# The moving operand of the split matmuls read as two interleaved halves, with weight columns stored even ones first

## The reference

```python
h = rms_norm(x) @ w_ff1            # 1024 -> 4096
x = x + square(relu(h)) @ w_ff2    # 4096 -> 1024
```

```python
def swiglu_ffn(h, w_gu, w_down):
    a, b = jnp.split(h @ w_gu, 2, axis=-1)   # 1024 -> 2 x 2816
    return (jax.nn.silu(a) * b) @ w_down     # 2816 -> 1024
```

## Time and profile before

| | |
|---|---|
| median of 3 runs | 1878.97 us (1878.77 to 1880.35) |
| profiled execution, its own time | 1878.69 us |
| its span | 1876.9 us |
| matmul records | 9754, each with a weight load |
| TensorE, weight loads, VectorE, ScalarE, GpSimd busy | 1868.9, 1591.5, 1420.3, 901.9, 222.7 us |
| HBM traffic | 190 GB/s over the span |

### The profile page before, as it was taken

How to read it: one execution, slowest core, us unless ns; L and a number is a source line. 1 busy time by engine, 2 the same in 40 slices (tenths; PEclk the granted TensorE clock), 3 DMA queues, 4 the chain that set the end, 5 groups by cost and what they waited for, 6 DMA issues and landing times.

```text
span 1876.9 us, 25424 instructions
## 1 busy us (share of the span) xinstructions
PE 1868.9 (100%) x9754; PEld 1591.5 (85%) x9754; DVE 1420.3 (76%) x1621; ACT 901.9 (48%) x990; POOL 222.7 (12%) x189
## 2 busy tenths in 40 slices
PE   9999999999999999999999999999999999999998
PEld 7888888888888888888898888888888898888887
DVE  7997866579868666776789887667766789887666
ACT  5564443444644344534545545444444555545443
POOL 0000000000001000000058230000000058230000
PEclk9999999999999999999999999999999999999999
DMA  8555555564556554555465456555655465455552
GB/s 305 191 178 209 181 193 188 179 216 180 185 199 222 192 193 165 213 191 189 157 194 180 164 198 225 186 191 182 213 183 186 172 194 180 157 202 207 187 182 109
DMA packets 52016, 357.40 MB, mean 190 GB/s; under 512 B 6552, under 2 KB 6688, under 8 KB 10080
## 3 DMA queue, kind: packets, MB, share of 16 engines
q1 hardware_dynamic: 47952, 341.93, 52.0%
q0 software_dynamic: 3696, 14.33, 2.6%
q10 hardware_dynamic: 288, 0.04, 0.0%
HBM read 354.15 MB, written 2.11 MB: 190 GB/s over the span
## 4 chain that ended last, share of the span: by engine, by line
PE 99%; issue 0%; DMA 0%; DVE 0%; ACT 0%; DVEq 0%; POOLq 0%; POOL 0%; SPq 0%; ACTq 0%
PE ps L234 24%; PE ps L309 14%; PE ps L310 14%; PE ps L317 14%; PE ps L239 13%; PE ps L196 4%; PE ps L198 3%; PE ps L197 3%; PE ps L2894 1%; PE ps L2895 1%; PE ps L2899 1%; PE ps L2639 1%; PE ps L214 0%; PE ps L221 0%; PE ps L215 0%; PE ps L413 0%
## 5 line engine op out<-in xcount | busy, mean ns | idle before, releaser
L172 DVE TENSOR_TENSOR w_lo<-raw,w_hi 128x2048 fp32r<-128x2048 f32 x312 | 716.5, 2302 | 239.4 <-ACT w_hi L165 238.5
L165 ACT ACTIVATE w_hi<-raw 128x2048 fp32r<-128x2048 f32 x312 | 596.8, 1915 | 499.3 <-PE ps L317 239.8
L234 PE MATMUL ps<-a,w_hi 128*128 128x512 f32 x2016 | 479.8, 390 | 0.0
L234 PEld LDWEIGHTS ps<-a,w_hi 128*128 128x128 f32 x2016 | 374.5, 188 | 75.4
L239 PEld LDWEIGHTS ps<-a,w_lo 128*128 128x128 f32 x2016 | 258.5, 191 | 9.8
L239 PE MATMUL ps<-a,w_lo 128*128 128x256 f32 x2016 | 261.5, 283 | 0.0
L309 PE MATMUL ps<-w_hi,a 128*128 128x512 f32 x592 | 233.2, 394 | 0.0
L310 PE MATMUL ps<-w_hi,a 128*128 128x512 f32 x592 | 230.6, 390 | 0.0
L309 PE MATMUL ps<-w_hi,mix 128*128 128x512 f32 x576 | 225.1, 391 | 0.0
L310 PE MATMUL ps<-w_hi,mix 128*128 128x512 f32 x576 | 225.0, 391 | 0.0
L317 PE MATMUL ps<-w_lo,a 128*128 128x512 f32 x592 | 146.3, 389 | 0.0
(11 more groups left out here) (416 smaller groups left out, 2065.2 us busy)
## 6 DMA issues: line engine op xcount, KB each, us to landing
raw<-in_w_b SPq DMA_DIRECT2D x198, 1024.0 KB, 4.8
raw<-in_w_a SPq DMA_DIRECT2D x124, 1024.0 KB, 4.9
rows<-in_post_gains POOLq DMA_DIRECT2D x6, 512.0 KB, 6.0
rows<-in_rows_a POOLq DMA_DIRECT2D x2, 1028.0 KB, 7.8
raw<-in_w_a SPq DMA_DIRECT2D x4, 512.0 KB, 6.8
rows<-in_rows_a POOLq DMA_DIRECT2D x2, 1024.0 KB, 6.8
x<-in_x SPq DMA_DIRECT2D x2, 512.0 KB, 5.3
a_gates<-bias_line POOLq DMA_DIRECT2D x2, 512.0 KB, 6.3
```

The lines of the kernel that those rows point to most:

```text
L165: act.activation(k.w_hi[s], k.raw[:, s, :], ACT.Copy).then_inc(k.hi_ready, 1)
L172: dve.tensor_tensor(k.w_lo[s], k.raw[:, s, :], k.w_hi[s].bitcast(F32), ALU.subtract).then_inc(k.lo_ready, 1)
L234: pe.matmul(both, hi[:, kt, n * P:(n + 1) * P], k.a[:, :, kt, :], start=kt == 0, stop=False)
```

## The change

It alters the order in which the moving operand is read, and what has to follow from that.

- Two helpers describe views. `halves_in_turn` turns n columns (a n) into (n a): the moving columns go 0, n/2, 1, n/2 + 1, and so on. `in_pairs` views the output as pairs of neighbours, so output column j still goes to word j.
- t chunks: the host packs each group of 512 weight columns with the even ones first and the odd ones after them, so reading the halves in turn gives columns 0, 1, 2, 3 and the output is where it was.
- f chunks: the moving tokens are read as token 0, 128, 1, 129, so a result has the tokens of both tiles in turn. `sum_halves` takes the place of `halves` and its reduction: it reads PSUM in an order that puts the tokens back, and writes its output 128 words apart. L2109 and L2451 read PSUM with a step of two words.
- The values chunk (L2760) is f-packed and keeps its contiguous order, with its three matmuls written out.
- Number, shape and order of instructions, semaphores, buffers and DMAs stay as they are.

The diff, cut to its core:

```diff
+def halves_in_turn(ap):
+    return ap.rearrange("p (a n) -> p n a", a=2)
+def in_pairs(ap):
+    return ap.rearrange("p (n a) -> p n a", a=2)
 def product(pe, out, a, b, first, end):
-    pe.matmul(out, a[0], b[0], start=first, stop=False)
-    pe.matmul(out, a[0], b[1], start=False, stop=False)
-    return pe.matmul(out, a[1], b[0], start=False, stop=end)
+    out, hi, lo = in_pairs(out), halves_in_turn(b[0]), halves_in_turn(b[1])
+    pe.matmul(out, a[0], hi, start=first, stop=False)
+    pe.matmul(out, a[0], lo, start=False, stop=False)
+    return pe.matmul(out, a[1], hi, start=False, stop=end)
...
 def f_pair(k, pe, c, bank, count):
-        both = k.ps[:, bank + n, :].rearrange("p (a n) -> p a n", a=2)
+        both = k.ps[:, bank + n, :].rearrange("p (s n t) -> p s n t", s=2, t=TT)
         for kt in range(KT):
-            pe.matmul(both, hi[:, kt, n * P:(n + 1) * P], k.a[:, :, kt, :], start=kt == 0, stop=False)
+            pe.matmul(both, hi[:, kt, n * P:(n + 1) * P], k.a[:, :, kt, :].rearrange("p s (t n) -> p s n t", t=TT),
+                      start=kt == 0, stop=False)
...
-        high = k.ps[:, bank + n, 0:SEQ]
+        high = in_pairs(k.ps[:, bank + n, 0:SEQ])
         for kt in range(KT):
-            end = pe.matmul(high, lo[:, kt, n * P:(n + 1) * P], k.aH[:, kt, :], start=False, stop=kt == KT - 1)
+            end = pe.matmul(high, lo[:, kt, n * P:(n + 1) * P], halves_in_turn(k.aH[:, kt, :]), start=False, stop=kt == KT - 1)
...
-def halves(k, bank):
-    return k.ps[:, bank:bank + 2, :].rearrange("p b (a n) -> p b n a", a=2)
+def sum_halves(dve, dst, k, bank):
+    return dve.tensor_reduce(dst.rearrange("p f (t n) -> p f n t", t=TT),
+                             k.ps[:, bank:bank + 2, :].rearrange("p b (s n t) -> p b n t s", s=2, t=TT), AX.X, ALU.add)
...
 def t_late(...):
-                w = hi[:, i, h * step:(h + 1) * step]
-                pe.matmul(out(tt, h), a[0], w, start=first and i == 0, stop=False)
-                pe.matmul(out(tt, h), a[1], w, start=False, stop=False)
+                w = halves_in_turn(hi[:, i, h * step:(h + 1) * step])
+                pe.matmul(in_pairs(out(tt, h)), a[0], w, start=first and i == 0, stop=False)
+                pe.matmul(in_pairs(out(tt, h)), a[1], w, start=False, stop=False)
...
-                act.activation(flat(qkF[:, 0:2, :]), k.ps[:, mixed_bank[7], :], ACT.Copy).then_inc(f_evicted.sem, 1)
+                act.activation(by_tile(qkF[:, 0:2, :]), k.ps[:, mixed_bank[7], :].rearrange("p (f n t) -> p f t n", f=2, t=TT), ACT.Copy).then_inc(f_evicted.sem, 1)
...
 def t_pack(w, width):
     n = CH // width
+    w = w.reshape(w.shape[0], width // 512, 256, 2).transpose(0, 1, 3, 2).reshape(w.shape)
     return [w[i:i + n * P].reshape(n, P, width).transpose(1, 0, 2).reshape(P, CH) for i in range(0, w.shape[0], n * P)]
```

More of the change, by code:

```diff
@@ L218, in f_chunk @@
         for n in range(tiles):
-            out = k.ps[:, bank, n * SEQ:(n + 1) * SEQ]
+            out = in_pairs(k.ps[:, bank, n * SEQ:(n + 1) * SEQ])
             for kt in kts:
-                end = pe.matmul(out, lo[:, kt, n * P:(n + 1) * P], act(kt)[0], start=False, stop=n == tiles - 1 and kt == kts[-1])
+                end = pe.matmul(out, lo[:, kt, n * P:(n + 1) * P], halves_in_turn(act(kt)[0]), start=False, stop=n == tiles - 1 and kt == kts[-1])
     end.then_inc(k.chunk_done, 1)
@@ L316, in t_late @@
             for i, kt in enumerate(kts):
-                ins = pe.matmul(out(tt, h), act(kt)[0][:, tt * P:(tt + 1) * P], lo[:, i, h * step:(h + 1) * step],
-                                start=False, stop=end and i == len(kts) - 1)
+                ins = pe.matmul(in_pairs(out(tt, h)), act(kt)[0][:, tt * P:(tt + 1) * P],
+                                halves_in_turn(lo[:, i, h * step:(h + 1) * step]), start=False, stop=end and i == len(kts) - 1)
     ins.then_inc(k.chunk_done, 1)
@@ L2759, in _ @@
                         a = [x[:, tt * P:(tt + 1) * P] for x in aop(kt)]
-                        ins = product(pe, k.ps[:, tt, 0:VALUES], a, [w[:, kt, :] for w in values_w], kt == 0, kt == KT - 1)
+                        out, w = k.ps[:, tt, 0:VALUES], [w[:, kt, :] for w in values_w]
+                        pe.matmul(out, a[0], w[0], start=kt == 0, stop=False)
+                        pe.matmul(out, a[0], w[1], start=False, stop=False)
+                        ins = pe.matmul(out, a[1], w[0], start=False, stop=kt == KT - 1)
                 ins.then_inc(k.chunk_done, 1)
@@ L2898, in branch @@
                         for kk in range(4):
-                            ins = pe.matmul(out[kk // 2], yH[:, 4 * q + kk, cols], lo[:, kk, :], start=False, stop=kk % 2 == 1)
+                            ins = pe.matmul(in_pairs(out[kk // 2]), yH[:, 4 * q + kk, cols], halves_in_turn(lo[:, kk, :]),
+                                            start=False, stop=kk % 2 == 1)
                         if tt == 0:
```

29 lines of the change are left out of this document (15 added, 14 removed).

## The result

The changed kernel takes 1802.98 us (median of 4 runs, 1802.7 to 1805.19) against 1878.88 for the kernel before in the same session: a ratio of 0.9597, 95% interval 0.958 to 0.9613. That is 75.9 us less. The forecast was 1801. The profiled execution spans 1801.0 us, at a granted clock of 1.0 as before. Lines moved down by 10 to 17: L234 is L245, L239 is L251, L309, L310 and L317 are L322, L323 and L330, L196 to L198 are L207 to L209, L172 and L165 are L182 and L175, L2301 is L2314, L1037 is L1050, L2451 and L2109 are L2464 and L2122; all the sums are at L257.

A forecast was written before the change was run, and what follows sets the result against it. TensorE was taken as the bound, its matmuls filling 1868.9 of 1876.9 us. Terms of -69.2, -18.4 and +10 made -77.6 us, so 1878.97 fell to 1801 us; range 1782 to 1910, held at 0.8.

The forecast's parts named there:

- The toll: TensorE matmuls with contiguous moving operands: some 12 ns extra per matmul, the same at 512 and 256 columns.
- parts 1 and 2 of the forecast: TensorE matmuls: 6528 of 512 columns gain 10.6 ns each, 69.2 us; 2304 of 256 gain 8, 18.4 us.
- part 2: 2304 TensorE matmuls 256 columns wide: 8 ns less each, 18.4 us (12.4 to 24.4); the weight load may end last.
- the pace of the weight load: TensorE reads: two moving streams at 1.2 columns per ns, like the weights, avoid collisions; up to 10.6 ns per matmul.
- The f32 records of the earlier trace: L1444's plain f32 matmuls: eight records at 216.3 ns each, taken as showing no toll, against 226.9.
- part 3: VectorE's 128 PSUM reductions, now writing 128 words apart: cost 0 (0 to 8.5 us).
- part 4: Evictions L2109 (ScalarE) and L2451 (VectorE) reading every second PSUM word: cost 0; doubled they would add 2.6 us.
- part 6: Seven stretches where VectorE is 98% busy: 10 us of TensorE's gain given back.
- A: Rival on TensorE's matmuls: the toll is fixed and nothing changes, 1879 us; chance 0.18.
- B: Rival on moving-column fetches: every hop costs in full, 1668 us more, 3547 us; chance 0.14.
- C: Rival on TensorE's reads: streams collide with weight loads more often, 1973 us, or 1910 at a third; chance 0.13.
- the f32 pace: Moving-column fetches: 0.845 ns a column, from L1444's f32 matmuls, against 0.42; taken as the worst case.

The follow-up runs named there:

- e5_distance: Changed kernel with the two words read in turn 2 to 128 words apart, a different distance per source line; 1805.64 us, one run.
- e6_ways: Changed kernel with moving columns read round 4, 8 or 16 parts, or with plain steps of 2, 4 or 8 words; 2724.92 us.
- e8_load_order: Kernel before, contiguous moving operand, with some weight loads (t_late's second high matmul, f_pair's low one) reading every second word; 1888.16 us.
- e4_sum_order: Changed kernel with VectorE's sums writing contiguously and reading PSUM with a step of two words; 1804.74 us, ratio 0.9611.
- e1_t_back: Changed kernel with the t chunks put back to contiguous weight columns, no host reordering, tokens still paired; 1842.68 us.
- e2_f_back: Changed kernel with the f chunks, their sums and evictions put back, tokens contiguous, weights still paired; 1842.09 us.
- e12_light_after: Changed kernel with both convolutions' taps cut to 16 of 256 tokens, so VectorE has less to do; 1792.0 us, ratio 0.9537.
- e10_runs: Changed kernel reading two places in turn by runs of 2, 4, 8 or 16 words, or single words 3 or 6 apart; 2143.22 us.
- e7_small_loads: Kernel before, contiguous moving operand, with some stationary operands narrowed to 64 or 32 columns instead of 128; 1882.18 us.
- e9_row_order: Changed kernel with the r_tokens row stored tile by tile, so VectorE reads it contiguously and its store is in 4-byte pieces; 1828.69 us.

## Why the forecast came out

**The toll (parts 1 and 2 of the forecast).** Right in size. Taken were 10.6 ns at 512 columns and 8 at 256; the rows give 11.3 and 8.1 within their rounding, and the trace's middle spacings 227 to 216 and 120 to 112. The 111.3 ns at 256 columns lie below the 114 that part 2 worked out for the weight load alone; that figure is too high, as of the 24 loads at L1470 the second starts 231 ns after the first and the others follow at 109. Together 69.2 + 18.4 = 87.6 us were forecast in the matmuls, and TensorE's busy time fell by 89.2.

**The mechanism.** Wrong in its reason, right in its contrast. The step said that two streams at the pace of the weight load do not collide with it. e5_distance shows that the streams may be 4 words apart; e6_ways shows 16 parts, walking slower still, at 434 ns; e8_load_order lets the load walk at the stream's pace, and the spacing goes from 227 to 236 and 224 and not to 216. What holds in all runs: contiguous 512 wide reads take 224 to 236 ns in the middle of their groups, 8 to 20 more than pairs, with 32, 64 or 128 columns loaded beside them; single words from two places 4 words apart or a larger power of two, in turn, take 216, and then a stepped load beside costs none either. That the contiguous toll comes from the load at all is likely, since it moves with it, and not shown: no run streams without one. The f32 records of the earlier trace rows were a hint at a slower stream, not at pairs. And they move 256 columns in their 216.3 ns. The rule that the forecast takes from the Trainium skill, "TensorE: Matmul & The Clock Gate", Part 1, N / 2.4 GHz + 2.5 ns, gives 109 ns for 256 columns and 216 for 512, so the forecast is wrong that these records agree with it; the paired 512 wide F32R ones (215.6) do. So the step that gave the sign, "the pace of the weight load", was not the cause, and that the number agreed was luck in part.

**The sums (part 3).** Right: 1223 ns with scattered writes, and no price in the time (e4_sum_order).

**The evictions (part 4).** The one on ScalarE stays at 628 ns. The one on VectorE went from 692 to 868 ns, 0.35 us in all, but by the same cause as the multiplies, whose operands are all in SBUF and which take 754 to 860 in the branch (L2401). Missed was this cause: 40 x 146 ns at L2314, 8 x 163 at L1050 and eight more, 62 to 176 ns each, make 8.2 us, about what VectorE's busy time rose by (1420.3 to 1428.2), none of it in the forecast. How much of it reaches the time was not measured by itself.

**Given back (part 6).** 10 us were taken, 13.3 measured. The place was half right: waits for `w_lo` appeared (L330, 3.2 us), but the longest row is L1439 behind L1095, also VectorE's. e1_t_back and e2_f_back put more of the loss on the t side, e12_light_after puts 9 us of it on VectorE.

**The rivals.** A, a fixed toll, fell in the result already, and e8_load_order shows the toll moving without the F32R form changing. B, every hop costs, gave 3547 us and fell for this order; that hops cost is true of nearly every other order tried. Its working took the f32 pace, 0.845 ns a column; four parts of 512 columns take 291 / 512 = 0.57, a plain step of 4 words 460 / 512 = 0.90. The Trainium skill, "Advanced Engine Details and Errata", Memory Cachelines, has lines of 16 bytes and a penalty for going to another line at each access. The step between 2 and 4 words agrees with the size, and 434 to 460 ns for plain steps of 4 and 8 words with the penalty. Two lines in turn, 216 ns, are an exception that it does not have, and a plain step of 2 words, which hits each line twice, takes 450 ns all the same. C, more collisions, gave 1910 to 1973 us and fell in the result. Runs of neighbours are slower (237 to 325 ns, e10_runs), but whether by collisions with the load or by the hop itself no run separates.

**Open.** Which part of the fetch makes two lines in turn free, and what sets the series of 226 to 236 ns through which a contiguous stream settles. e7_small_loads is mixed at 512 columns, 8 parts are slower than 16, and no simple rule gives 268 and 217 ns for distances 3 and 6. Why VectorE's stepped read is slower beside paired reads was shown as a fact (e9_row_order, e2_f_back), not explained. An output in PSUM that hops as well was not tried. No version that computes the whole result was faster than the kernel after.

## What to carry to other kernels

Where TensorE is full, each matmul on F32R operands brings its own weight load, and the spacing at 512 columns is 227 ns instead of 216, reading the moving operand as single words in turn from two places 4 to 256 words apart (powers of two were tried), with the host's packing or the view of the result putting the order back, took the 11 ns away; try exactly that order, since four and more parts, plain steps and runs of neighbours take 21 to 299 ns more than the pairs' 216. Look first at how much another engine has left in the stages where both are full: 13 of 89 us were given back here, at least 9 of them to waits for VectorE. Before making a stepped operand contiguous, look at the store that fills it: 6 us more on a 1 KB store, landing five times, cost 26 us, 8 of them because the granted clock fell at the waits.

## What the runs showed of the hardware that was not expected

- The spacing of contiguous 512 wide moving streams of F32R words depends on the loads around them: 227 ns with contiguous loads, 236 and 224 in turn where every other load is stepped, 229 and 231 where every other load has 32 columns; a paired stream is at 216 with contiguous and stepped loads.
- After other loads a contiguous stream needs some five matmuls, at 226 to 236 ns, to settle at 227 again (L317 in e8_load_order).
- At 256 columns a contiguous stream is at 120 ns with either load, a paired one at 112 with a contiguous load and 120 with a stepped one.
- The gain does not need a distance: 4, 8, 16, 64, 128 and 256 words all give 215 to 216 ns, 2 words 230. Over 504 columns, 6 words give 217 and 3 words 268.
- Going round 4, 8 and 16 parts takes 291, 515 and 433 ns; steps of 2, 4 and 8 words 450, 460 and 434; two places by runs of 2, 4, 8 and 16 words 325, 254, 240 and 237.
- VectorE's multiply with a step of two words in one SBUF operand takes 754 to 868 ns while TensorE reads in pairs and 676 to 695 beside contiguous reads; with that operand contiguous it takes 676 to 693 beside paired reads too.
- A reduction over PSUM with its result written 128 words apart, or read with a step of two, takes the same 1.22 us.
- At waits of 3.2 to 4.3 us TensorE's granted clock fell to 0.50 for 3.4 to 6.8 us, and eight 512 wide matmuls took 446 ns each instead of 216 (e9_row_order).
